# Expert loads in another order, three norms by output halves, and four small moves

## The reference

```
first block
  x += 0.5 * swiglu(rms_norm(x), ffn1)                     # hidden 2816
  p = rms_norm(x) @ w_in                                    # q, k, v and the inputs of the RWKV-7 branch
  x += concat(stick_breaking_attention(...), rwkv7(...)) @ w_out
  x += 0.5 * swiglu(rms_norm(x), ffn2)
second block (x and a context of 256 tokens)
  h = modulate(rms_norm(x)), differential attention over 512 keys, a Fourier branch, two gates
  x += g1 * ((sigmoid(ga) * (attn @ w_ao) + sigmoid(gf) * (four @ w_fo)) @ w_o)
  t = modulate(rms_norm(x))
  for e in 16 experts: y = (silu(t @ w1[e]) * (t @ w3[e])) @ w2[e];  acc += gate[:, e] * y
  out = rms_norm(x + g2 * acc)
```

## Time and profile before

| | us |
|---|---|
| median of 3 runs | 1167.74 |
| lowest, highest | 1167.27, 1175.66 |
| profiled execution | 1168.66 |
| its span, first to last instruction | 1166.8 |
| TensorE busy | 1110.8 (95%) |
| DVE busy, ACT busy | 594.6, 446.4 |
| mean granted clock of TensorE | 0.992 |
| moved by DMA | 254.88 MB, mean 218 GB/s |

### The profile page before, as it was taken

How to read it: one execution, slowest core, us unless ns; L and a number is a source line. 1 busy time by engine, 2 the same in 40 slices (tenths; PEclk the granted TensorE clock), 3 DMA queues, 4 the chain that set the end, 5 groups by cost and what they waited for, 6 DMA issues and landing times.

```text
span 1166.8 us, 20530 instructions
## 1 busy us (share of the span) xinstructions
PE 1110.8 (95%) x8828; PEld 906.8 (78%) x8828; DVE 594.6 (51%) x799; ACT 446.4 (38%) x561; POOL 24.6 (2%) x29
## 2 busy tenths in 40 slices
PE   6999999999998998999999999999999899989896
PEld 6999997999877747999999999988999643434342
DVE  5645555688644276554556473277567542212122
ACT  6333434753431125433335332366574421111112
POOL 0000000000212100000000000000000000000000
PEclk9999999899999999999999999999999999999999
DMA  9655556444485843555655243332346869999994
GB/s 343 230 184 180 183 190 196 134 145 145 159 297 199 290 166 123 182 190 192 192 180 181 73 145 115 118 129 81 102 137 258 332 250 422 421 422 421 421 421 189
DMA packets 119992, 254.88 MB, mean 218 GB/s; under 512 B 6113, under 2 KB 91377, under 8 KB 107378
## 3 DMA queue, kind: packets, MB, share of 16 engines
q1 hardware_dynamic: 118722, 249.14, 59.9%
q10 hardware_dynamic: 1200, 4.71, 1.1%
HBM read 252.78 MB, written 1.06 MB: 218 GB/s over the span
## 4 chain that ended last, share of the span: by engine, by line
PE 80%; DMA 9%; DVE 6%; ACT 4%; issue 1%; SPq 0%; ACTq 0%; DVEq 0%
PE ps L685 54%; PE ps L666 24%; DMA arena<-in_w_exp_up 9%; ACT arena L1383 2%; PE ps L1136 1%; DVE ring_r L2007 1%; DVE arena L2058 1%; DVE arena L2194 1%; DVE arena L2084 1%; ACT L1383 1%; ACT arena_r L1383 1%; DMA cst<-in_consts 0%; DVE arena L2072 0%; PE ps L673 0%; DVE ring_r L1912 0%
## 5 line engine op out<-in xcount | busy, mean ns | idle before, releaser
L685 PE MATMUL ps<-hall_r,arena_r 128*128 128x256 f32 x1760 | 326.6, 283 | 5.4 <-DVE hall_r L1918 2.6
L1912 DVE TENSOR_TENSOR ring_r<-ring,arena_r 128x2048 fp32r<-128x2048 f32 x90 | 205.9, 2290 | 180.6 <-ACT arena_r L1383 178.5
L685 PE MATMUL ps<-arena_r 128*128 128x256 f32 (+1 forms) x1216 | 284.2, 323 | 1.2 <-DVE arena_r L2298 1.2
L685 PEld LDWEIGHTS ps<-hall_r,arena_r 128*128 128x128 f32 x1760 | 275.8, 190 | 8.0 <-issue 4.3
L1383 ACT ACTIVATE arena_r<-ring 128x2048 fp32r<-128x2048 f32 x100 | 190.8, 1914 | 158.0 <-PE ps L685 153.2
L685 PE MATMUL ps<-hall_r,ring_r 128*128 128x256 f32 x880 | 247.3, 281 | 0.0
L685 PEld LDWEIGHTS ps<-arena_r 128*128 128x128 f32 x1216 | 202.6, 188 | 19.7 <-DVE arena_r L2298 1.4
L1383 ACT ACTIVATE arena<-ps 128x512 f32<-128x512 f32 (+3 forms) x133 | 77.9, 599 | 339.3 <-PE ps L685 192.8
L666 PE MATMUL ps<-arena 64*64 64x32 f32 (+7 forms) x2232 | 191.6, 303 | 11.2 <-DMA arena<-in_w_exp_up 5.7
L666 PEld LDWEIGHTS ps<-arena 128*64 128x64 f32 (+3 forms) x2232 | 118.7, 142 | 70.7 <-issue 61.7
L685 PEld LDWEIGHTS ps<-hall_r,ring_r 128*128 128x128 f32 x880 | 168.8, 192 | 0.9
(11 more groups left out here) (247 smaller groups left out, 1004.4 us busy)
## 6 DMA issues: line engine op xcount, KB each, us to landing
ring<-in_w_in SPq DMA_DIRECT2D x35, 1024.0 KB, 5.2
arena<-in_w_exp_down SPq DMA_DIRECT2D x32, 1024.0 KB, 17.8
ring<-in_w_mod SPq DMA_DIRECT2D x24, 1024.0 KB, 5.8
ring<-in_ffn_gate SPq DMA_DIRECT2D x22, 1024.0 KB, 5.4
ring<-in_ffn_up SPq DMA_DIRECT2D x22, 1024.0 KB, 5.4
ring<-in_ffn_down SPq DMA_DIRECT2D x22, 1024.0 KB, 5.0
ring<-in_w_exp_gate SPq DMA_DIRECT2D x20, 1024.0 KB, 18.8
arena<-in_w_exp_up SPq DMA_DIRECT2D x16, 1024.0 KB, 21.6
```

What stands on the lines that cost most here:

```text
L685: m = pe.matmul(out_, w[i], h[j], start=start and i + j == 0, stop=stop and j == 1, skip_group_check=group)
L1912: tt(lo(n), slot(n), hi(n), ALU.subtract).then_inc(S("w_lo"), 1)
```

## The change

Four groups of edits:

1. Expert loads. `follow(pair, u, four, four_after)` replaces `expert_pair`. For turn n it first loads m = 0, 1, 2 of turn n + 2 (each waits for its use in turn n), then m = 3 to 11 of turn n + 1 (each waits for its use in turn n). So turn n + 2's first three stand ahead of turn n + 1's other nine. The last turns load nothing beyond turn 7; the last pair has a loop of its own.
2. Norms by halves, for n2, n3, n4 and their tile 1. The last product's order is tile 0, then tile 1's first 512 columns, then its second 512 (`last_first`); a semaphore `row_part` counts tile 0 and the first half of tile 1. `add_rows` adds tile 1's first half after that. ACT squares the halves one by one, with a small Identity between them that turns the first half's sum into the bias of the root. DVE scales tile 1 in two halves, and the transposes of the second half wait for the second. In the product of `N_O2` only the semaphore's name changes, not the order.
3. Start. The constant for ACT's first Sqrt is written by a memset on POOL, so ACT no longer waits for `ident_in` there. The low part of the very first weights is made in two halves of 128 columns (`first_low`): the first ahead of the norm columns, the second behind them; TensorE's first half product (f = 0) waits for the first, f = 1 for the second.
4. Order. On DVE low_in(8) moves ahead of the head norm of kk, and shifts 5 and 6 move ahead of low_in(9) and the masked products. On TensorE out_rows(N_WOUT, 0) is cut in two: f = 0 ahead of y_var, f = 1 behind it.

The diff, cut to its core:

```diff
@@ shared["each_" + what]
+            in_parts = {"ss": 4, "scaled": 3}
+            shared["each_" + what] = [
+                (f"{tag}_{what}", in_parts.get(what, count) if tag in ("n2", "n3", "n4") else count) for tag in tags]
@@ last_first
             if last:
-                return [(f, t) for t in range(TT) for f in fs]
-            return [(f, t) for f in fs for t in range(TT)]
+                return [(f, 0, (0, 1)) for f in fs] + [(f, 1, (h,)) for h in range(2) for f in fs]
+            return [(f, t, (0, 1)) for f in fs for t in range(TT)]
@@ SP, expert loads
-            def expert_pair(e0, pair, u):
-                for m in range(PAIR):
-                    ago = 2 if m < TWICE else 1
-                    sp.wait_ge(*W("w_used", nth(N_EXP + m - PAIR * ago + 1, pair, u, PAIR)))
-                    load_expert(m, e0, u)
+            def follow(pair, u, four, four_after):
+
+                if four_after is not None:
+                    for m in range(TWICE):
+                        sp.wait_ge(*W("w_used", nth(N_EXP + m + 1, pair, u, PAIR)))
+                        load_expert(m, four_after, u)
+                for m in range(TWICE, PAIR):
+                    sp.wait_ge(*W("w_used", nth(N_EXP + m + 1, pair, u, PAIR)))
+                    load_expert(m, four, 1 - u)
...
-            for m in range(TWICE, PAIR):
-                sp.wait_ge(*W("w_used", N_EXP + m + 1))
-                load_expert(m, 0, 1)
-            with sp.Fori(1, E // 4 - 1) as pair:
-                for u in range(2):
-                    expert_pair(pair * 4, pair, u)
+            with sp.Fori(0, E // 4 - 2) as pair:
+                follow(pair, 0, pair, pair + 1)
+                follow(pair, 1, pair + 1, pair + 1)
             sp.wait_ge(*W("rounds", 1))
             n_r = sp.value_load(n_rounds[0:1, 0:1].bitcast(U32), min_val=1, max_val=4)
-            with sp.Fori(E // 4 - 1, n_r * (E // 4)) as pair:
-                for u in range(2):
-                    expert_pair((pair % (E // 4)) * 4, pair, u)
+            with sp.Fori(E // 4 - 2, n_r * (E // 4) - 1) as pair:
+                follow(pair, 0, pair % (E // 4), (pair + 1) % (E // 4))
+                follow(pair, 1, (pair + 1) % (E // 4), (pair + 1) % (E // 4))
+            with sp.Fori(n_r * (E // 4) - 1, n_r * (E // 4)) as pair:
+                follow(pair, 0, pair % (E // 4), None)
@@ POOL
+            pool.memset(first_eps, EPS).then_inc(S("c_zero"), 1)
@@ PE, norm_transposes
                     for k in range(KT):
+                        if t == 1 and k == KT // 2 and tag in norm_after:
+                            pe.wait_ge(*W(tag + "_scaled", 3))
@@ PE, half product of the FFN
-                    split_weight(n, it, 6)
+                    if n == N_FFN1:
+                        pe.wait_ge(*W("first_lo", 1))
+                    else:
+                        split_weight(n, it, 6)
                     for f in range(2):
+                        if n == N_FFN1 and f == 1:
+                            split_weight(n)
@@ PE, last product (down; out_rows alike)
-                        if i == FFC - 1 and (f, t) == (1, 0):
-                            m.then_inc(S("tile_0"), 1)
+                        if i == FFC - 1 and (f, t + h) == (1, 1):
+                            m.then_inc(S("row_part"), 1)
@@ PE, w_out
-            out_rows(N_WOUT, 0)
+            out_rows(N_WOUT, 0, (0,))
             pe.wait_ge(*W("y_sq", 2))
             four(2, lambda o, k: mm(o, head_mean, sq[:, k, :]), "y_var")
+            out_rows(N_WOUT, 0, (1,))
             out_rows(N_WOUT, 1)
@@ ACT, norm, tile 1 of n2, n3, n4
+                    act.wait_ge(*(W(f"x_in{t}", 16) if first else W(norm_after[tag], 2 + t)))
+                    if t and not first:
+                        half, rest = x[:, t, 0:512], x[:, t, 512:1024]
+                        f(xn[:, t, 0:512], half, ACT.Square, accum_out=halves_ss[:, 0:1]).then_inc(S(tag + "_ss"), 1)
+                        act.wait_ge(*W(tag + "_ss", 2))
+                        f(half_mean[:, 0:1], halves_ss[:, 0:1], ACT.Identity, scale=1.0 / D, bias=EPS_COL).then_inc(
+                            S(tag + "_ss"), 1)
+                        act.wait_ge(*W(norm_after[tag], 4))
+                        f(xn[:, t, 512:1024], rest, ACT.Square, accum_out=halves_ss[:, 1:2]).then_inc(
+                            S(tag + "_ss"), 1)
+                        act.wait_ge(*W(tag + "_ss", 4))
+                        f(rstd[:, t:t + 1], halves_ss[:, 1:2], ACT.Sqrt, scale=1.0 / D,
+                          bias=half_mean[:, 0:1]).then_inc(S(tag + "_root"), 1)
@@ ACT, start
-            act.wait_ge(*W("ident_in", 16))
-            fetch(ACT.Sqrt)
+            act.wait_ge(*W("c_zero", 1))
+            f(small[:, 70:71], first_eps, ACT.Sqrt)
@@ DVE, norm_rows
-                    ts(o, src, rstd[:, t:t + 1], None, ALU.mult).then_inc(S(tag + "_scaled"), 1)
+                    for part in ((slice(0, 512), slice(512, 1024)) if t and tag != "n1" else (slice(0, D),)):
+                        ts(xn[:, t, part], x[:, t, part], rstd[:, t:t + 1], None, ALU.mult).then_inc(
+                            S(tag + "_scaled"), 1)
@@ DVE, add_rows
+                parts_of = {"x1_done": 0, "x2_done": 2, "x3_done": 4}
+                for t, h in ((0, 0), (0, 1), (1, 0), (1, 1)):
+                    v.wait_ge(*(W("row_part", parts_of[tag] + t + 1) if t + h < 2 else W("w_used", used)))
+                    s = slice(h * 512, (h + 1) * 512)
+                    stt(x[:, t, s], ps[:, 4 + 2 * t + h, :], scale, x[:, t, s], ALU.mult, ALU.add).then_inc(S(tag), 1)
@@ DVE, start
+            def first_low(g):
+                half_ = slice(g * P, (g + 1) * P)
+                whole = slot(N_FFN1).rearrange("p (k n) -> p k n", k=KT)
+                tt(lo_cols(N_FFN1)[:, :, half_], whole[:, :, half_], hi_cols(N_FFN1)[:, :, half_],
+                   ALU.subtract).then_inc(S("w_lo" if g else "first_lo"), 1)
+
             norm_rows("n1")
-            split(N_FFN1)
+            v.wait_ge(*W("w_hi", 1))
+            first_low(0)
...
             norm_cols_lo("n1", lambda k: V("norm_ffn1", k))
+            first_low(1)
@@ DVE, w_in stage
             m.then_inc(S("bonus_prod"), 1)
+            low_in(8)
             v.wait_ge(*W("kk_norm", 1))
...
             tt(k_bar, kf, w_inv, ALU.mult).then_inc(S("k_bar"), 1)
-            low_in(8)
+            shift(5)
+            shift(6)
             low_in(9)
...
-            shift(5)
-            shift(6)
             low_in(10)
```

More of the change, by code:

```diff
@@ L193, in build @@
                                   ("prod", FFC, ("f1", "f2")), ("hid_hi", FFC, ("f1", "f2"))):
-            shared["each_" + what] = [(f"{tag}_{what}", count) for tag in tags]
+            in_parts = {"ss": 4, "scaled": 3}
+            shared["each_" + what] = [
+                (f"{tag}_{what}", in_parts.get(what, count) if tag in ("n2", "n3", "n4") else count) for tag in tags]
         sems, base = {}, {}
@@ L478, in build @@
         rt = lambda j, n=32: A(8, n, 32 * j)
+        first_eps = small[:, 71:72]
         EPS_COL, LNX_COL = C("eps")[:, 0:1], C("eps")[:, 1:2]
@@ L706, in down @@
                         normed("ctx")
-                    for f, t in last_first(i == FFC - 1, range(2)):
-                        for h in range(2):
+                    for f, t, hs_ in last_first(i == FFC - 1, range(2)):
+                        for h in hs_:
                             m = mm3(ps[:, 4 + 2 * t + h, :],
@@ L736, in ffn, with out_rows @@
                 down(FFC - 1)
-            def out_rows(n0, c):
+            def out_rows(n0, c, fs=range(2)):
                 weight(n0 + c)
-                for f, t in last_first(c == 3, range(2)):
+                for f, t, hs_ in last_first(c == 3, fs):
                     lhs = mix[c // 2][:, 2 * (c % 2) + f, :]
-                    for h in range(2):
+                    for h in hs_:
                         m = mm(ps[:, 4 + 2 * t + h, :], lhs[:, t * P:(t + 1) * P],
@@ L1220, in _ @@
                 pe.wait_ge(*W("y_mix_lo", c + 1))
-                for f, t in last_first(c == 3, range(2)):
+                for f, t in [(f, t) for t in range(TT) for f in range(2)] if c == 3 else [
+                        (f, t) for f in range(2) for t in range(TT)]:
                     for h in range(2):
@@ L1391, in norm @@
                 for t in range(TT):
[L1392 to L1399 removed]
+                    first = tag == "n1"
+                    act.wait_ge(*(W(f"x_in{t}", 16) if first else W(norm_after[tag], 2 + t)))
[11 more added lines that the diff above has]
+                          bias=half_mean[:, 0:1]).then_inc(S(tag + "_root"), 1)
+                    else:
+                        f(xn[:, t, :], x[:, t, :], ACT.Square, accum_out=ssum[:, t:t + 1]).then_inc(
+                            S(tag + "_ss"), 1)
+                        act.wait_ge(*W(tag + "_ss", t + 1))
```

(13 more changed lines are left out.)

30 lines of the change are left out of this document (9 added, 21 removed).

## The result

The changed kernel takes 1157.02 us (median of four runs, 1155.15 to 1162.5), the kernel before on the same chip 1168.62. The ratio is 0.9894, 95% interval 0.9865 to 0.9923, so no change is ruled out: 12.4 us less by the ratio, 11.6 by the two medians, where 10.9 were forecast. The profiled execution took 1155.15 around a span of 1153.3, so 13.5 less than the profiled one of before.

The account below looks back on a forecast made before the run. TensorE's own work was taken as four fifths of the span, DMA a tenth, the rest waits for DVE and ACT. Waits of 7.4 us plus clock of 3.5 made 1168.66 - 10.9 = 1157.8 us, range 1152.5 to 1163.5.

Parts of the forecast that it names:

- Start: First products: TensorE starts a us earlier, then waits for the second half of the weights; gain 0.2 us (0 to 0.7).
- n2: Norm behind the first FFN: by halves, tile 1's transposes start at 202.85 instead of 204.06; gain 1.2 us (0.9 to 1.6).
- n3: Norm behind w_out, where the last product is fp32: the same arithmetic by halves; gain 1.25 us (0.5 to 1.4).
- n4: Norm whose chain is covered by 5.7 us of matmuls for the context's keys: gain nothing, 1.2 without that cover.
- w_in: Projections 8 and 9: their waits go, a 1.2 us wait for bonus_v comes; 1.65 us of waits, 1.6 of clock.
- w_out: y_var ahead of half of w_out: rw_out no longer late; 1.06 us of waits, 1.7 us of half clock.
- The clock: Half-clock stretches at the first FFN's norm, project 9 and w_out: 5.25 us together, two of three taken, 3.5 us.
- Expert loads: Expert stage: bytes 7.5 us ahead, but order costs turn 6 the same; only the last turn gains, 2.0 us.
- Rival 1: Expert stage: DMA alone sets the end, so moved bytes reach it; 7.5 us instead of 2.0, 1152.3; chance 0.10.
- Rival 2: Next wait takes the place: chains keep half of 4.1 us, no clock stretch won; 5.3 us, 1163.4; chance 0.20.
- Rival 3: Turn 6's second pair waits 3.0 us in one piece and the clock falls there; priced at 1180; chance 0.05.
- Rival 4: Expert loads bound to another wait, so no lead: sum 8.9 us, 1159.8, inside the forecast; no chance given.

Follow-up runs that it names:

- the five parts: Each part alone on the kernel before, ratios: expert loads 0.9985, DVE's order 0.9989, norms by halves 0.9975, y_var between w_out's halves 0.9972, start 0.9979.

## Why the prediction was right, point by point

The forecast was 1157.8 us, 1157.0 was measured. The mechanisms that gave it were the right ones in every stage. That the two numbers are only 0.8 us apart is partly luck: the interval is 3.4 us wide each way, and by the stages of the profiles the change gave 13.5 us, 2.6 more than the sum, nearly all of it in the clock and in w_in.

- **Start.** The mechanism held: ACT's slack ends at the landing of the gate weights (1.58 us of it, not 0.7), the product starts a us earlier, the end gains almost nothing. 0.2 forecast, 0.3 measured at equal clock. In the first trace of the changed kernel it is -0.1, since the first products began at 1.2 GHz; the same kernel had them at 2.4 the next time, and of the two traces of the kernel before one began at 1.2 as well, so this can't be laid to the change.
- **n2.** 1.2 forecast, 0.9 measured at equal clock. The reciprocal came at 202.27 (202.16 worked out, and the FFN ended 0.1 late), and the transposes gained the 1.2. The missing 0.3 went to a queue that the prediction did not follow: ACT issues three loads before its first column, and their last issue now ends 0.46 us behind the first transpose of tile 1, where it was 0.18 behind with the old norm at equal clock. TensorE waits 1.24 us for the first column instead of 0.97 at equal clock. To issue those loads elsewhere was not tried.
- **n3.** 1.25 forecast, 1.3 measured. **n4** was costed at nothing; the stretch from the second FFN's first product to n4's transposes is 193.4 us in all 13 traces, so nothing it is. The 0.3 us by which the changed kernel's first trace is shorter from there to turn 0 is not the change's: the unchanged kernel's second trace is shorter by the same.
- **w_in.** 3.25 forecast with the clock, 4.2 measured. The steps came in the forecast order: shifts ended at 261.3, low_in(9) at 263.5, bonus_v at 271.7, all 2.9 to 3.0 us ahead of their forecast times. Of this 2.7 is n2's gain. The other 0.3 is DVE's wait of 0.26 us ahead of the head norm, which low_in(8) now fills; the prediction named it and then let bonus_v keep its time. The half clock cost 1.8 to 1.9 rather than 1.6, so that TensorE too came to that wait 0.25 us earlier than forecast. More was missed behind: before, the mean squares of k waited 0.45 us for DVE's masked rows of v, which stand behind q's late reciprocal, and now do not (293.35 against 286.61).
- **w_out.** 2.76 forecast with the clock, 2.83 measured, in all six traces; no wait is left, rw_out has the slack of 1.6 us that was forecast.
- **The clock.** This was the only term given by chance: two of three stretches, 3.5 of 5.25 us. All three went: at each place the clock held in all six traces with the wait shortened, and fell in 18 of 21 cases without (5, 6 and 7 of 7). Taking two thirds was too careful by 1.8 us. But in the matmuls of 64 rows the clock falls or not without a cause that was found, which no step of the prediction held; the first traces of both kernels happened to be without it. This may be why the profiled difference, 13.5, is larger than 12.4 by the ratio, 11.6 between the medians and 10.7 against the median known ahead; it was not tested. It does make single parts of 1 to 3 us come out with intervals wider than themselves. By their ratios the five parts add up to 1.8 + 1.3 + 2.9 + 3.3 + 2.5 = 11.8 us, but each is known to some 2.3 us either way and the last is 0.3 by the traces, so the agreement with 12.4 says little.
- **What wakes the clock.** The prediction let n2's sixteen transposes count and n2 stay at 2.4 GHz. In the changed kernel n2 has 1.74 us of idleness, 3.3 us with nothing but transposes and a wait, and then full-rate matmuls, six times in six. The Trainium skill, "TensorE: Matmul & The Clock Gate", part 4, says that transposes do not count as TensorE being busy in the same way; by that rule the 5.05 us between the products would still have been a gap for the clock, and 9 us would have been the sum. (The 9 takes off all of n2's 1.95, of which the 10.9 held only two thirds; 9.6 would be consistent.) The runs do not bear the rule out. At n2 alone they don't tell whether transposes count or 5.05 us are merely short enough. The start tells: nothing but the sixteen transposes stands ahead of the first product, and in 8 of 13 traces that product is at full rate (0.35 or 0.36 us). In two of these, the loads alone and DVE's order alone, the clock rose while the transposes ran: they start 0.21 us apart at first and 0.11 at the end, and all sixteen take 3.4 us instead of 3.63. The one with DVE's order (timeline):

```profile
8.97 3.39 PE L673 MATMUL ps<-cst,arena 128*128 128x128 f32 x16 [8.97 <-DVE arena L1907]
...
14.14 0.36 PE L685 MATMUL ps<-hall_r,arena_r 128*128 128x256 f32 x1 [1.78 <-DVE hall_r L1918]
```

In the other five traces the first product is at half rate (0.55), so transposes can raise the clock and need not.
- **Expert loads.** 2.0 forecast, 2.0 measured, and by the mechanism told: bytes 7.5 us ahead, given back by order, waits in turn 6, none in turn 7. Its wait in the second pair of turn 6 was told as 3.0 and is 2.46. Rival 1, the moved bytes reach the end, was wrong of this kernel, but right of what the lead could be worth: with the three behind the nine the stage gains 7.4 to 7.8 us instead of 2.0, which is the 7.5 us of transfers. The prediction saw that order costs 5.5 and did not ask for a version that doesn't pay it.
- **The other rivals.** Rival 2 (the next wait takes the place) was true at bonus_v, where the sum had it, and for 0.3 us at n2, by another step than those it named. Its price halves the 4.1 us of three places while it names five; half of all 5.36 us would give 1164.0 instead of 1163.4. Rival 3 (the clock falls at turn 6's longer wait): granted 1.00 from 1025 to 1128 us in the changed kernel; with the loads alone it did fall there, for 3.4 us, and was hidden by the next transfer. That is one of the four traces with this wait (2.46 to 2.50 us). Its mechanism is real, its price is not: the transfers bound that turn. Rival 4 (no lead) fell by DMA's 0.99 from 926 on.

## What to carry to other kernels

Where DMA is the bound and weights have two buffers, lead and order are two things: load early while the queue would be idle, but once it is full issue in the order of use; here the same 3 MB of lead was worth 2.0 us in one order and 7.5 in the other. A wait of one or two us in front of TensorE costs its own length and at some places as much again in clock (18 of 21 cases at three places here), at others nothing (the waits of 1.0 to 1.4 us in the expert turns), so take the place's own record over several traces rather than one. When a chain is made shorter, follow also what an engine issues in between: 0.3 us stayed with ACT's three loads. And with a stretch that falls by chance, compare stages between traces by the same instructions; whole-run times hide gains of 1 to 4 us. Look at a second trace of the unchanged kernel before a few tenths are laid to the change.

## What the runs showed of the hardware

- The clock also falls in unchanged code, without a cause that was found: the matmuls of 64 rows in 8 of 13 traces, at a cost of 1.8 to 6.7 us. It fell in 5 of the 7 traces without a fall at project 9 and in 3 of the 6 with one, too few to say whether the one makes room for the other.
- Two profiles of the same kernel differ by 7.3 us (1166.8 and 1174.1), nearly all of it in clock.
- Transposes alone can raise the clock: in two traces it rose within the first sixteen (0.21 us apart, then 0.11), with no other matmul in front; in 5 of 13 it had not risen when the first product began.
- The first products of one kernel are at 1.2 GHz in one execution and at 2.4 in another (0.55 or 0.36 us for the first matmul): in the two traces of the kernel before, 0.36 at 14.03 and 0.55 at 14.09.
- The granted clock of a window can miss such a stretch: in the changed kernel it is 1.00 for 10 to 14 and for 14 to 18 us, where pairs of matmuls take 0.63 instead of 0.40. The trace's record of the clock begins only with the rise, here at 15.9 us (11.0 to 18.6 over the 13 traces), and what lies ahead of it is shown as 1.00. There the durations are the sign to go by.
- ACT's issues of three loads took 0.6 us each of its own time: in all 13 traces its first column behind n2 starts 0.04 to 0.21 us behind the last of them.
